# Moving the four gate tiles of the input projection into the weight ring, behind the retention value tiles

## The reference, cut to what matters

```python
z = h @ w_in
q, k, v, qi, ki, wi, rq, rk, rv, g = jnp.split(z, offs, axis=-1)
...
att = sparse_attend(q, k, v, idx, valid)      # idx: top-k of the indexer's scores
ret = retention(rope(rq), rope(rk), rv)       # by chunks of 128 tokens, with a state
y = concatenate([att, silu(g) * group_norm(ret)]) @ w_out
```

## Time and profile before

| | |
|---|---|
| median of 3 runs | 1702.93 us |
| lowest and highest | 1699.05 and 1705.05 us |
| span of the profiled execution | 1703.5 us |
| PE busy | 1627.4 us (96%) |
| DVE busy | 715.7 us (42%) |
| ACT busy | 432.0 us (25%) |
| POOL busy | 127.4 us (7%) |

### The profile page before, as it was taken

How to read it: one execution, slowest core, us unless ns; L and a number is a source line. 1 busy time by engine, 2 the same in 40 slices (tenths; PEclk the granted TensorE clock), 3 DMA queues, 4 the chain that set the end, 5 groups by cost and what they waited for, 6 DMA issues and landing times.

```text
span 1703.5 us, 27541 instructions
## 1 busy us (share of the span) xinstructions
PE 1627.4 (96%) x10137; PEld 1362.9 (80%) x10137; DVE 715.7 (42%) x1138; ACT 432.0 (25%) x697; POOL 127.4 (7%) x186
## 2 busy tenths in 40 slices
PE   7999999999999999999988989998989999999995
PEld 6999999999764889898663363334869999999995
DVE  3333323222323888888463244552153323332224
ACT  3433332121324000000120002331063333332123
POOL 0000000341220000000200010000140000000001
PEclk9999999999999999999999968999989999999998
DMA  4222222333222556566025543342112222222221
GB/s 178 87 86 86 80 82 69 115 104 92 71 64 78 165 176 183 177 175 222 14 65 171 164 131 98 110 121 80 62 36 88 86 81 80 85 86 72 87 82 61
DMA packets 73219, 176.88 MB, mean 104 GB/s; under 512 B 9681, under 2 KB 13778, under 8 KB 72914
## 3 DMA queue, kind: packets, MB, share of 16 engines
q1 hardware_dynamic: 67730, 164.20, 31.2%
q0 software_dynamic: 4576, 8.13, 1.5%
q10 hardware_dynamic: 864, 3.91, 0.6%
HBM read 169.11 MB, written 7.09 MB: 103 GB/s over the span
## 4 chain that ended last, share of the span: by engine, by line
PE 90%; DVE 5%; ACT 3%; DMA 1%; issue 1%; ACTq 0%; POOL 0%; DVEq 0%; PEldq 0%
PE ps L311 88%; PE ps L314 2%; ACT scr L729 1%; ACT xbuf L729 1%; DMA xbuf<-in_x_t 1%; DVE rbuf L1011 1%; DVE scr L1020 1%; DVE scr L1180 0%; ACT x_high L729 0%; DVE mxb L1135 0%; DVE w_low L950 0%; DVE big L1011 0%; DVE lg L1149 0%; DVE small L1171 0%; ACT wring L729 0%
## 5 line engine op out<-in xcount | busy, mean ns | idle before, releaser
L311 PE MATMUL ps<-x_high,w_high 128*128 128x280 f32 x1408 | 417.8, 297 | 16.8 <-DVE x_low L956 10.7
L311 PE MATMUL ps<-x_high,w_low 128*128 128x280 f32 x1408 | 415.9, 295 | 0.0
L311 PE MATMUL ps<-x_low,w_high 128*128 128x280 f32 x1408 | 414.1, 294 | 0.0
L950 DVE TENSOR_TENSOR w_low<-wring,w_high 128x1024 fp32r<-128x1024 f32 (+1 forms) x136 | 162.8, 1198 | 520.2 <-ACT w_high L729 520.1
L311 PEld LDWEIGHTS ps<-x_high,w_high 128*128 128x128 f32 x1408 | 269.0, 191 | 22.1 <-issue 13.9
L311 PEld LDWEIGHTS ps<-x_low,w_high 128*128 128x128 f32 x1408 | 269.4, 191 | 0.0
L311 PEld LDWEIGHTS ps<-x_high,w_low 128*128 128x128 f32 x1408 | 267.9, 190 | 0.0
L729 ACT ACTIVATE w_high<-wring 128x1024 fp32r<-128x1024 f32 (+1 forms) x136 | 140.6, 1035 | 434.2 <-PE ps L311 428.8
L311 PE MATMUL ps<-xbuf,wring 128*128 128x280 f32 x928 | 239.5, 410 | 1.2 <-DVE sc L1077 0.9
L311 PEld LDWEIGHTS ps<-xbuf,wring 128*128 128x128 f32 x928 | 172.4, 192 | 42.2 <-issue 4.1
L311 PE MATMUL ps<-h_low,w_high 128*128 128x280 f32 x704 | 205.4, 292 | 0.0
(11 more groups left out here) (155 smaller groups left out, 1422.1 us busy)
## 6 DMA issues: line engine op xcount, KB each, us to landing
dring<-in_k_pool SPq DMA_DIRECT2D x128, 256.0 KB, 2.8
dring<-in_v_pool SPq DMA_DIRECT2D x128, 256.0 KB, 2.8
wring<-in_wg SPq DMA_DIRECT2D x44, 512.0 KB, 3.5
wring<-in_wu SPq DMA_DIRECT2D x44, 512.0 KB, 3.5
wring<-in_wd SPq DMA_DIRECT2D x32, 512.0 KB, 3.6
wring<-in_w_in SPq DMA_DIRECT2D x29, 512.0 KB, 3.8
wring<-in_wd SPq DMA_DIRECT2D x16, 384.0 KB, 3.1
wring<-in_w_out SPq DMA_DIRECT2D x8, 512.0 KB, 3.8
```

Source lines behind the costliest of these rows:

```text
L311: return nc.tensor.matmul(out, lhs, rhs, start=start, stop=stop, **kw)
L950: v.tensor_tensor(wl[:, to, 0:n], w4[:, s, 0:n], wh[:, to, 0:n].bitcast(F32), ALU.subtract) \
```

## The change

The four gate weights are loaded by the weight ring: SP's loop of four RV weights becomes a loop of eight weights (RV, then G) on slots 0 to 3 twice. The view `gw` of the page ring and SP's wait for `sg_done` ahead of the value pages go. PE runs eight projection tiles in a row and waits for all 33 tiles of `z` before the transposes; `gate_tile` and its waits go. ACT evicts the last four with Silu in the same loop; `gate` goes. DVE waits for `z_done` instead of `sg_done` ahead of the chunks. `OUT_W` counts one use more of each slot.

```diff
--- before.py
+++ after.py
@@ -156,7 +156,6 @@
         wh, wl = (w[:, :].rearrange("p (s n) -> p s n", s=2) for w in (w_high, w_low))
         w4 = wring[:, :].rearrange("p (s n) -> p s n", s=4)
         kv = dring[:, 0:4096].rearrange("p (s n) -> p s n", s=8)
-        gw = dring[:, 0:4096].rearrange("p (s n) -> p s n", s=4)
         st = dring[:, 4096:5632].rearrange("p (s n) -> p s n", s=3)
 
         s_buf = tiles(scr, 2)
@@ -263,12 +262,8 @@
                     weight(j, w_in[bass.ds(i * 2 + FIRST + 2 + j, 1)].rearrange("a p n -> (a p) n"))
                     for s in range(CUT[j], CUT[j + 1]):
                         kv_page(s % 8, i * NPAGE + NPAGE + s, k_pool)
-            for j in range(4):
-                weight(j, w_in[RV + j])
-            for j in range(4):
-                for s in (2 * j, 2 * j + 1):
-                    sp.wait_ge(sem(f"kv_free{s}"), 2 * NB)
-                sp.dma_start(gw[:, j, :], w_in[G + j]).then_inc(sem("gw_in"), 16)
+            for j in range(8):
+                weight(j % 4, w_in[RV + j])
 
             sp.wait_ge(sem("index_done"), 1)
             sp.dma_start(scr[:, 0:2 * T], rope_tab).then_inc(sem("rope_in"), 16)
@@ -276,7 +271,6 @@
             sp.dma_start(k_o, z[:, K:K + 4, :]).then_inc(sem("kvi_out"), 16)
             sp.dma_start(v_o, z[:, V:V + 4, :]).then_inc(sem("kvi_out"), 16)
             sp.dma_start(i_o, z[0:64, KW, :]).then_inc(sem("kvi_out"), 16)
-            sp.wait_ge(sem("sg_done"), 4)
             with loop(sp, NB * 2, [(f, 1) for f in kvf]) as i:
                 for s in range(8):
                     kv_page(s, i * 8 + s, v_pool)
@@ -496,11 +490,11 @@
                 last = mm(ps[0:NS, 7, hp * 64:hp * 64 + 64], z[:, K + hp, SMP:TL],
                           qb[:, hp, :, :].rearrange("p b n -> p (b n)"))
             last.then_inc(sem("p16_full"), 1)
-            for j in range(4):
-                weight(j)
+            for j in range(8):
+                weight(j % 4)
                 pe.wait_ge(sem("z_done"), zdone.up())
-                wide(j % 2, w4[:, j, :], KT, x).then_inc(sem(f"w_free{j}"), 1)
-            pe.wait_ge(sem("z_done"), G)
+                wide(j % 2, w4[:, j % 4, :], KT, x).then_inc(sem(f"w_free{j % 4}"), 1)
+            pe.wait_ge(sem("z_done"), ZT)
 
             k = 0
             for src in (V, RV):
@@ -526,18 +520,6 @@
                     last = mm(ps[:, 2 * (u % 2) + a, 0:HALF], c("rot"), z[:, RQ + u, a * HALF:(a + 1) * HALF])
                 last.then_inc(sem("rot_full"), 1)
 
-            def gate_tile(j, p):
-
-                wide(p, gw[:, j, :], KT, x).then_inc(sem("g_full"), 1)
-
-            pe.wait_ge(sem("gw_in"), 64)
-            pe.wait_ge(sem("p16_done"), 1)
-            gate_tile(0, 3)
-            pe.wait_ge(sem("zs_done"), 7)
-            gate_tile(1, 0)
-            pe.wait_ge(sem("sg_done"), 1)
-            gate_tile(2, 3)
-
             pe.wait_ge(sem("mask_used"), 1)
             pe.wait_ge(sem("mx_done"), 1)
             for g in range(2):
@@ -545,8 +527,6 @@
             last.then_inc(sem("mxt_full"), 1)
             pe.wait_ge(sem("diag_done"), 1)
             mm(ps[:, 4, 0:256], ones, diag).then_inc(sem("mxb_full"), 1)
-            pe.wait_ge(sem("sg_done"), 3)
-            gate_tile(3, 3)
             pe.wait_ge(sem("psum_done"), 1)
             for g in range(2):
                 last = mm(ps[:, 5, g:g + 1], mx[:, g * P:(g + 1) * P], ones[:, 0:1])
@@ -856,9 +836,9 @@
                 last = ev(lgt[0:NS, :, 512 + hp * 8:512 + hp * 8 + 8],
                           ps[0:NS, 7, hp * 64:hp * 64 + 64].rearrange("p (b n) -> p b n", b=NB), scale=AD ** -0.5)
             last.then_inc(sem("p16_done"), 1)
-            for j in range(4):
-                act.wait_ge(wf[j].sem, wf[j].up())
-                ev(halves(z[:, RV + j, :]), pair(j % 2)).then_inc(sem("z_done"), 1)
+            for j in range(8):
+                act.wait_ge(wf[j % 4].sem, wf[j % 4].up())
+                ev(halves(z[:, RV + j, :]), pair(j % 2), ACT.Copy if j < 4 else ACT.Silu).then_inc(sem("z_done"), 1)
             k = 0
             for src in (V, RV):
                 for t in range(6):
@@ -869,17 +849,9 @@
                     ev(o, ps[0:n, k % 4, :]).then_inc(sem("tr_done"), 1)
                     k += 1
 
-            def gate(j, p):
-                act.wait_ge(sem("g_full"), j + 1)
-                ev(halves(z[:, G + j, :]), pair(p), ACT.Silu).then_inc(sem("sg_done"), 1)
-
-            gate(0, 3)
-            gate(1, 0)
-            gate(2, 3)
             for b in range(NB):
                 act.wait_ge(sem("sub_done"), b + 1)
                 ev(lgt[:, b, :], lgt[:, b, :], ACT.Exp).then_inc(sem("sp_done"), 1)
-            gate(3, 3)
             for cn in range(6):
                 n = P if cn < 4 else (TAIL, NS)[cn - 4]
                 act.wait_ge(sem("bag_done"), cn + 1)
@@ -1187,7 +1159,7 @@
                     .then_inc(sem("mixr_done"), 1)
 
             dve.wait_ge(sem("ret_in"), 16)
-            dve.wait_ge(sem("sg_done"), 4)
+            dve.wait_ge(sem("z_done"), ZT)
             dve.wait_ge(sem("rope_done"), 8)
             gam = c("gam")
             for cn in range(5):
@@ -1367,7 +1339,7 @@
             norm(2)
 
 
-OUT_W = [FF_W[0] + 3 + NB + 1, FF_W[1] + 2 + NB + 1, FF_W[2] + 2 + 1, FF_W[3] + 2 + 1]
+OUT_W = [FF_W[0] + 3 + NB + 2, FF_W[1] + 2 + NB + 2, FF_W[2] + 2 + 2, FF_W[3] + 2 + 2]
 
 
 def _tables():
```

## The result

The changed kernel takes 1728.57 us (median of 4 runs, 1725.15 to 1730.52) beside 1702.41 us for the kernel before. The ratio is 1.0155, with a 95% interval of 1.0137 to 1.0174: it is slower by 26 us. The profiled execution of after has a span of 1728.8 us and a time of 1730.52, so some 1.7 us lie around the span. By that the profiled execution of before, with its span of 1703.5, was among its slower ones too (some 1705 us), and the two spans can be compared as they stand: 25.3 us apart.

The account below looks back on a forecast made before the run. PE, busy 96%, sets the end until 829.89, then mostly DVE from 831.14 to 884.45. From the median 1702.93 us, 30.45 − 6.4 + 1.0 = +25.0 us gives 1728 us, range 1718 to 1736.

Parts of the forecast that it names:

- The delay of the mask: Gate tiles ahead of the mask transposes on PE make every step behind them start later: +30.45 us.
- The wait at the end of the gates: DVE's 6.90 us wait after its maxima for PE's two transposes, queued behind the third gate tile, shrinks: −6.4 us.
- the cold steps: Two small PE steps before the retention chunks run at the lower clock after a longer hole: +1.0 us.
- The ring and the queue: Gate weights waiting for weight-ring slots, and transfers SP moves past them, are hidden by PE's eight tiles: 0 us.
- the part behind the chunks' start: Sign: span after the retention chunks begin; a difference from before of more than 8 us would make the prediction wrong.
- The selection: Rival: DVE's selection ends after PE's arrival at the mask transposes, making the gate tiles free: 1696.5 us, chance 0.02.
- The ring did not hold TensorE up: Rival denied here: late gate weights expose 5 us at each of four tiles, 20 us: 1748 us, chance 0.02.
- The clock rose within the first chunk: Against the rival that the low clock lasts through the first two retention chunks, +12 us: 1740 us, chance 0.08.
- the later stretch at the lower level: Rival: the low-clock stretch from 988 to 1036 runs at full level, gaining at most 15.6 us: 1712 us, chance 0.05.

Follow-up runs that it names:

- the place alone: Kernel before with only TensorE's four gate tiles moved ahead of the transposes, page ring and SP's program untouched: 1726.73 us, ratio 1.0152.
- two tiles: Kernel before, page ring kept, with two gate tiles ahead of the transposes and two behind: 1710.03 us, ratio 1.0055.
- the interleaved kernel: Changed kernel with VectorE's softmax chain early, mask behind the third value tile, rotations between gate-tile halves and transposes, rotary table loaded before weights: 1686.85 us, ratio 0.9918.

## Why the prediction was right, point by point

**The delay of the mask, +30.45 us.** Measured 30.23 (831.14 to 861.37 on VectorE), and the runs with the place alone and with two tiles show that it is this delay, not the ring.

**The wait at the end of the gates, −6.4, and the cold steps, +1.0.** VectorE's wait fell from 6.90 to 0.84 us, −6.06. It holds the two transposes, 0.66 us at the lower clock instead of 0.38. The spread took 1.22 us instead of 0.70, and with it the part from the end of that wait to the chunks grew by 0.49. Together −5.6, where I had −5.4.

**Not in my sum within the stretch:** VectorE's rotations, mask and maxima were 0.76 us shorter, most of it at the first two rotations: in before the rotary matmuls ran there at a lowered clock (0.64 granted from 832 to 836), here at the full one (1.00 from 860 to 864). Hence 23.9 us (30.23 − 5.57 − 0.76) instead of 25.0 at the chunks.

**The ring and the queue, 0.** Right for all that I listed: the gate weights, the table, the outputs and the pages were not waited for. What I had not listed is the rest of SP's program: the 2.0 us of the last stores come with the kernels that load the gates by the ring and not with the place alone, so this term was too small by them.

**Not in my sum outside the stretch:** −0.7 us on the way to the output projection and +2.1 us behind it, 2.0 of them in the last stores. The −0.7 should not be read as an effect: that part took 289.52 us in the interleaved kernel and 284.39 in the same with four waits more on SyncE. I said that the part behind the chunks' start would differ by less than 8 us; it differs by 1.4. So the forecast of 1728 against 1728.57 owes a part of its closeness to luck: the stretch gave 1.1 us less than forecast, the rest of the kernel 1.4 more. I also set the span of 1703.5 beside the median of the times as if it were a time; with the 1.7 us around it that execution lay some 2 us above the median, not 0.6. The forecast was counted from the median and does not change by it.

**The rivals.** The selection was ready long before the mask's transposes, as read. The ring did not hold TensorE up. The clock rose within the first chunk by the same instructions as in before (0.77 granted from 912 to 916), and the later stretch at the lower level remained (0.54 from 1012 to 1060, where before has 0.51 from 988 to 1036). The hole's clock was worth 0.8 us in the hole's own two steps (0.28 + 0.52); the chunks' start at the lower clock, 2.6 us, was there before.

## What to carry to other kernels

Before moving independent work on an engine that runs in order, look at who is waiting behind the new place. Work that nobody waits for belongs behind the step that a ready engine waits for; as far as that engine's chain then covers it, it is free. The same tiles cost 26 us ahead of the mask and gained 14 to 17 us against the kernel before when the waiting engine's steps were cut in between them. TensorE's busy share of 96% told nothing of this; the idle time of the other engine, and what ended it, did.

## What the runs showed that I had not expected

The turns of SyncE's first output loop cost about 0.88 us in before, 1.10 in the changed kernel and 1.07 with four waits put back, with the same instructions in the loop; since the kernel ends behind these stores, this is 1.5 to 2 us of its time. The 16 stores took the same time in every profile of one family of kernels, so it goes with the program and not with the execution. In these profiles it goes with the number of SyncE's instructions (2800, 2796 and 2798); whether that number, the place of the loop or something else in the program sets it stays open.
